# Small parameter loads moved from SP's queue to ACT's, and a new order of the first steps, in a two-layer decoder trunk

## The reference, cut to what matters

```python
for l in range(DEPTH):
    h = rmsnorm(x, g_mix[l])
    z = h @ w_in[l]                      # 1024 x 3080: conv b, c, v; q, k, v; 8 forget logits
    ...
    q = rmsnorm(q, g_q[l]); k = rmsnorm(k, g_k[l])
    log_f = log_sigmoid(f_logit + b_f[l])
    y_fox = forgetting_attention(q, k, v, log_f)
    x = x + concat([y_conv, y_fox]) @ w_out[l]
    m = rmsnorm(mem, g_mem[l])
    x = x + mem_cross_attention(rmsnorm(x, g_xa[l]), m, ...) @ w_xo[l]
    ...                                   # layer 0: dense SwiGLU; layer 1: top-2-of-8 expert SwiGLU
```

## Time and profile before

| | |
|---|---|
| median of 3 runs | 1467.98 us (1465.68 to 1470.63) |
| profiled execution | 1475.52 us, of it 1474.0 us span |
| PE busy | 1396.1 us (95%) |
| DVE, ACT, POOL busy | 1000.9, 803.3, 77.7 us |
| moved by DMA | 386.28 MB, mean 262 GB/s |
| first matmul, first product with a z slot | 13.72 us, 28.26 us |

### The profile page before, as it was taken

How to read it: one execution, slowest core, us unless ns; L and a number is a source line. 1 busy time by engine, 2 the same in 40 slices (tenths; PEclk the granted TensorE clock), 3 DMA queues, 4 the chain that set the end, 5 groups by cost and what they waited for, 6 DMA issues and landing times.

```text
span 1474.0 us, 19381 instructions
## 1 busy us (share of the span) xinstructions
PE 1396.1 (95%) x7593; PEld 1188.5 (81%) x7593; DVE 1000.9 (68%) x779; ACT 803.3 (54%) x702; POOL 77.7 (5%) x82
## 2 busy tenths in 40 slices
PE   5899998999999999985999999999999999999998
PEld 4897666899988997564888888888888888888786
DVE  4437345545457465334798897888878888889888
ACT  4335124334344433223686777777867777677674
POOL 3000000000001000002000000000000000000400
PEclk9999899999999998996999999999999999999999
DMA  9323044464459321413898999999999999999994
GB/s 304 127 88 115 29 172 165 136 208 163 150 200 379 129 87 58 176 56 136 324 388 345 385 346 394 389 341 400 351 380 367 357 393 380 351 382 345 406 399 181
DMA packets 126627, 386.28 MB, mean 262 GB/s; under 512 B 7938, under 2 KB 61806, under 8 KB 126574
## 3 DMA queue, kind: packets, MB, share of 16 engines
q1 hardware_dynamic: 114686, 365.08, 66.5%
q0 software_dynamic: 3168, 11.54, 2.0%
q10 hardware_dynamic: 8720, 8.91, 1.7%
HBM read 369.78 MB, written 15.73 MB: 262 GB/s over the span
## 4 chain that ended last, share of the span: by engine, by line
PE 68%; DVE 11%; DMA 8%; ACT 6%; issue 5%; POOL 1%; SPq 1%; DVEq 0%; ACTq 0%; POOLq 0%
PE bank L1458 41%; PE bank L1454 13%; PE bank L1455 12%; DVE wl L1035 5%; DMA ring<-in_we_gate 4%; DMA ring<-in_we_down 3%; ACT wh L730 3%; DVE wl L1016 2%; PE bank L1860 1%; DVE xl L1041 1%; ACT xh L918 1%; ACT wh_third L730 1%; DMA rows_of<-xn,rows 1%; DVE scratch L1162 1%; DVE scratch L1145 0%
## 5 line engine op out<-in xcount | busy, mean ns | idle before, releaser
L1035 DVE TENSOR_TENSOR wl<-ring,wh 128x2816 fp32r<-128x2816 f32 (+1 forms) x127 | 400.3, 3171 | 61.3 <-PE bank L1458 35.2
L730 ACT ACTIVATE wh<-ring 128x2816 fp32r<-128x2816 f32 (+1 forms) x128 | 336.8, 2633 | 124.8 <-DMA ring<-in_we_down 43.0
L1016 DVE TENSOR_TENSOR wl<-ring,wh 128x3072 fp32r<-128x3072 f32 (+2 forms) x53 | 158.2, 2988 | 101.1 <-ACT wh L716 91.9
L1454 PE MATMUL bank<-wh,xh 128*128 128x512 f32 x528 | 200.9, 381 | 22.0 <-ACT wh L730 14.5
L1035 DVE TENSOR_TENSOR wl<-ring,wh_third 128x2816 fp32r<-128x2816 f32 (+1 forms) x64 | 187.1, 2923 | 33.4 <-PE bank L1458 25.2
L1455 PE MATMUL bank<-wh,xl 128*128 128x512 f32 x528 | 199.2, 377 | 0.0
L1458 PE MATMUL bank<-wl,xh 128*128 128x512 f32 (+1 forms) x768 | 194.9, 375 | 0.0
L730 ACT ACTIVATE wh_third<-ring 128x2816 fp32r<-128x2816 f32 (+1 forms) x64 | 155.7, 2432 | 52.7 <-DMA ring<-in_we_up 21.0
L716 ACT ACTIVATE wh<-ring 128x3072 fp32r<-128x3072 f32 (+1 forms) x52 | 128.3, 2469 | 97.2 <-DMA ring<-in_w_xq 46.4
L1458 PEld LDWEIGHTS bank<-wl,xh 128*128 128x128 f32 x768 | 141.9, 188 | 18.4
L1454 PEld LDWEIGHTS bank<-wh,xh 128*128 128x128 f32 x528 | 99.9, 189 | 44.9 <-issue 19.4
(11 more groups left out here) (271 smaller groups left out, 2032.1 us busy)
## 6 DMA issues: line engine op xcount, KB each, us to landing
ring<-in_we_gate SPq DMA_DIRECT2D x64, 1408.0 KB, 7.9
ring<-in_we_up SPq DMA_DIRECT2D x64, 1408.0 KB, 8.2
ring<-in_we_down SPq DMA_DIRECT2D x56, 1536.0 KB, 9.0
ring<-in_w_in SPq DMA_DIRECT2D x16, 1536.0 KB, 8.8
ring<-in_w_gate SPq DMA_DIRECT2D x6, 1536.0 KB, 7.4
ring<-in_w_up SPq DMA_DIRECT2D x6, 1536.0 KB, 6.7
ring<-in_w_down SPq DMA_DIRECT2D x6, 1536.0 KB, 7.0
rows_of<-zeros ACTq DMA_DIRECT2D x1, 8704.0 KB, 46.2
```

The lines of the kernel that those rows point to most:

```text
L730: nc.scalar.activation(wh_in_pass(j, n), ring[:, slot, 0:n], ACT.Copy).then_inc(high_ready, 1)
L1016: nc.vector.tensor_tensor(wl[:, j, 0:n], ring[:, slot, 0:n], wh[:, j, 0:n].bitcast(F32), ALU.subtract).then_inc(low_ready, 1)
L1035: nc.vector.tensor_tensor(wl[:, j % 2, 0:n], ring[:, j % NSLOT, 0:n], wh_in_pass(j, n).bitcast(F32), ALU.subtract).then_inc(low_ready, 1)
L1454: nc.tensor.matmul(dst, x_high, w_high, start=first, stop=False)
```

## The change

SP's queue now holds x, z0, z1, the memory, z2, z3. The 18 small DMAs are the first instructions of ACT's queue, ahead of the load of its function table. PE transposes x before it waits for the 18 and transposes `vrows`. On ACT the split of z0 comes behind `input_high`, then the squares of x, the split of z1 and the squares of the memory. On DVE the low part of z0 comes first, then the diagonal of the roots (`root_diagonal`), the low part of z1, and the normalising of the memory. The memory's transposes on PE move from ahead of qk0 to behind `roots_spread` after qk1; DVE copies them behind the forget gate's first steps. The names of the banks are put in the new order; with it qk0 and qk1 get other banks, "f" and "qk2" still share one. `memraw` and one of two scratch areas for squares change places.

```diff
@@ -66,9 +66,10 @@
 def layer_results(layer):
 
     names = [f"xT{i}" for i in range(4)] + ["f"]
+    names += ["qk0", "qk1", "rr"]
     if layer == 0:
         names += [f"mT{i}" for i in range(4)]
-    names += ["qk0", "qk1", "rr", "qk2", "qk3", "v0", "v1", "ssqk"]
+    names += ["qk2", "qk3", "v0", "v1", "ssqk"]
     names += [f"conv{i}" for i in range(3)] + [f"bq{i}" for i in range(4)] + [f"conv{i}" for i in range(3, 6)]
     names += [f"s{h}" for h in range(8)]
     names += ["mk0", "mk1", "mv0", "mv1", "ssc", "ssmk"] + [f"pt{h}" for h in range(8)]
@@ -242,13 +243,13 @@
         zc = part(0, 12, S)
         zqk = part(3072, 8, S)
         sq = part(5120, 8, S)
-        memraw = part(5120, TT, D)
+        memraw = part(1024, TT, D)
         sc = part(5120, FH, 3 * P)
         osq = part(5120, TT * FH, HD)
         rdiag = part(12544, TT, P)
         rfull = part(12800, S)
         rsquare = part(13056, S)
-        mixjunk = part(1024, TT, D)
+        mixjunk = [part(5120, TT, D), part(1024, TT, D)]
         xajunk = part(5120, TT, D)
         ffnjunk = part(0, TT, D)
         vtok = part(8192, 2, FH * HD)
@@ -517,25 +518,7 @@
                     slot_free(fill_names[n - NSLOT])
                 dst = ring[:, n % NSLOT, 0:k * c].rearrange("p (k c) -> p k c", k=k)
                 sp.dma_start(dst, src).then_inc(slot_filled[n % NSLOT], 16)
-                if n == 0:
-
-                    for nm, src in (("mix", g_mix), ("xa", g_xa), ("mem", g_mem), ("ffn", g_ffn), ("cv", g_conv_out),
-                                    ("fox", g_fox_out), ("xq", g_xq), ("xk", g_xk)):
-                        r, k = vec[0, nm], L * src.shape[1] // P
-                        sp.dma_start(vrows[r:r + k, :], src.rearrange("l (k p) -> (l k) p", p=P)).then_inc(params_loaded, 16)
-                    r = vec[0, "tap"]
-                    sp.dma_start(vrows[r:r + 12 * L, :], conv_w.rearrange("l j (k p) -> (l j k) p", p=P)).then_inc(params_loaded, 16)
-                    for nm, src in (("q", g_q), ("k", g_k)):
-                        r = vec[0, nm]
-                        for half in range(2):
-                            sp.dma_start(vrows[r:r + L, half * HD:half * HD + HD], src).then_inc(params_loaded, 16)
-                    for l in range(L):
-                        sp.dma_start(wf[:, KT * l:KT * l + KT], w_in[l][:, ICOLS - FH:ICOLS].rearrange("(k p) c -> p k c", p=P)).then_inc(params_loaded, 16)
-                    r = vec[0, "bf"]
-                    sp.dma_start(vrows[r:r + L, :].rearrange("l (a h) -> l a h", h=FH),
-                                 b_f.unsqueeze(1).to_broadcast([L, P // FH, FH])).then_inc(params_loaded, 16)
-                    sp.dma_start(wr[:], w_router[0].rearrange("(k p) c -> p k c", p=P)).then_inc(params_loaded, 16)
-                    sp.dma_start(brow[:], b_router[0:1, :].to_broadcast([P, NE])).then_inc(params_loaded, 16)
+                if n == 1:
                     sp.dma_start(memraw, mem[0].rearrange("(t p) d -> p t d", p=P)).then_inc(mem_loaded, 16)
 
             gu_rows = [w[0].rearrange("e (k p) c -> p (e k) c", p=P) for w in (we_gate, we_up)]
@@ -689,6 +672,23 @@
         @block.scalar
         def _(act):
             steps = [0]
+            for nm, src in (("mix", g_mix), ("xa", g_xa), ("mem", g_mem), ("ffn", g_ffn), ("cv", g_conv_out),
+                            ("fox", g_fox_out), ("xq", g_xq), ("xk", g_xk)):
+                r, k = vec[0, nm], L * src.shape[1] // P
+                nc.scalar.dma_start(vrows[r:r + k, :], src.rearrange("l (k p) -> (l k) p", p=P)).then_inc(params_loaded, 16)
+            r = vec[0, "tap"]
+            nc.scalar.dma_start(vrows[r:r + 12 * L, :], conv_w.rearrange("l j (k p) -> (l j k) p", p=P)).then_inc(params_loaded, 16)
+            for nm, src in (("q", g_q), ("k", g_k)):
+                r = vec[0, nm]
+                for half in range(2):
+                    nc.scalar.dma_start(vrows[r:r + L, half * HD:half * HD + HD], src).then_inc(params_loaded, 16)
+            for l in range(L):
+                nc.scalar.dma_start(wf[:, KT * l:KT * l + KT], w_in[l][:, ICOLS - FH:ICOLS].rearrange("(k p) c -> p k c", p=P)).then_inc(params_loaded, 16)
+            r = vec[0, "bf"]
+            nc.scalar.dma_start(vrows[r:r + L, :].rearrange("l (a h) -> l a h", h=FH),
+                         b_f.unsqueeze(1).to_broadcast([L, P // FH, FH])).then_inc(params_loaded, 16)
+            nc.scalar.dma_start(wr[:], w_router[0].rearrange("(k p) c -> p k c", p=P)).then_inc(params_loaded, 16)
+            nc.scalar.dma_start(brow[:], b_router[0:1, :].to_broadcast([P, NE])).then_inc(params_loaded, 16)
             nc.scalar.preload_act_table_set("natural_log_exp_and_others")
 
             def then_wait(ins):
@@ -753,34 +753,32 @@
 
             for l in range(L):
 
-                if l == 0:
-                    act.wait_ge(x_loaded, 16)
-                else:
+                if l == 1:
                     act.wait_ge(consts_ready, 1)
                     nc.scalar.dma_start(rows_of.rearrange("(p a) (b c) -> p (a b) c", p=P, c=256),
                                         zeros[:].unsqueeze(1).to_broadcast([P, (2 * NE + 1) * (D // 256), 256])
                                         ).then_inc(rows_cleared, 16)
                     nc.scalar.preload_act_table_set("natural_log_exp_and_others")
                     high_of(l, "z", 0)
-                    mean_square(l, 0, "d", mixjunk, 0)
+                    mean_square(l, 0, "d", mixjunk[1], 0)
                 if l == 0:
-                    for t in range(TT):
-                        mean_square(l, t, None, mixjunk, 0)
                     act.wait_ge(params_loaded, 16 * NPARAMS)
                     nc.scalar.activation(wide(wf_wide[0][:, 0]), wf_each(0), ACT.Copy).then_inc(wf_split, 1)
-                    high_of(0, "z", 0)
                     act.wait_ge(*taken(0, "vec"))
                 input_high(l, "xT", "mix")
                 if l == 1:
-                    mean_square(l, 1, "d", mixjunk, 0)
+                    mean_square(l, 1, "d", mixjunk[1], 0)
                     high_of(l, "z", 1)
                 if l == 0:
+                    high_of(0, "z", 0)
+                    for t in range(TT):
+                        mean_square(l, t, None, mixjunk[0], 0)
+                    high_of(0, "z", 1)
                     act.wait_ge(mem_loaded, 16)
                     for t in range(TT):
                         nc.scalar.activation(memT[:].rearrange("p k s -> p (k s)")[:, t * D:t * D + D], memraw[:, t, :],
                                              ACT.Square, scale=D ** -0.5,
                                              accum_out=msq[:, 2 + t:3 + t]).then_inc(meansq_ready, 1)
-                    high_of(0, "z", 1)
 
                 for i in range(4):
                     act.wait_ge(*taken(l, f"qk{i}"))
@@ -1079,16 +1077,13 @@
                     dve.wait_ge(*taken(0, "vec"))
                 input_low(l, "xT", "mix")
                 if l == 0:
+                    low_of(0, "z", 0)
+                    root_diagonal(l, "mix", 0, rdiag)
+                low_of(l, "z", 1)
+                if l == 0:
                     normalise(l, "mem", memraw, 2, memraw)
-                    low_of(0, "z", 0)
-                low_of(l, "z", 1)
-
-                root_diagonal(l, "mix", 0, rdiag)
-                if l == 0:
-                    for i in range(4):
-                        dve.wait_ge(*full(l, f"mT{i}"))
-                        nc.vector.tensor_copy(memT[:, 2 * i:2 * i + 2, :].rearrange("p k s -> p (k s)"), bank(l, f"mT{i}")[:]
-                                              ).then_inc(take(l, f"mT{i}"), 1)
+                else:
+                    root_diagonal(l, "mix", 0, rdiag)
                 for i in range(4):
                     dve.wait_ge(*full(l, f"qk{i}"))
                     nc.vector.tensor_copy(zqk[:, 2 * i:2 * i + 2, :].rearrange("p a s -> p (a s)"), bank(l, f"qk{i}")[:]
@@ -1109,6 +1104,11 @@
                         dve.wait_ge(*taken(l, "rr"))
                         then_wait(nc.vector.reciprocal(erow[:], rsquare[0:16, :]))
                         nc.vector.tensor_scalar(erow[:], erow[:], EPS, None, ALU.mult).then_inc(erow_ready, 1)
+                        if l == 0:
+                            for b in range(4):
+                                dve.wait_ge(*full(l, f"mT{b}"))
+                                nc.vector.tensor_copy(memT[:, 2 * b:2 * b + 2, :].rearrange("p k s -> p (k s)"), bank(l, f"mT{b}")[:]
+                                                      ).then_inc(take(l, f"mT{b}"), 1)
                     if i == 2:
                         dve.wait_ge(fln_ready, l + 1)
                         then_wait(nc.vector.tensor_tensor(fz[:, 3, :], fz[:, 3, :], fz[:, 2, :], ALU.subtract))
@@ -1580,21 +1580,18 @@
                 return i * BANK, min(i * BANK + BANK, DFF)
 
             pe.wait_ge(ident_ready, 1)
-            pe.wait_ge(params_loaded, 16 * NPARAMS)
```

(11 more changed lines are left out.)

## The result

The changed kernel takes 1476.32 us in the median of 5 runs (1475.6 to 1483.29), the kernel before 1467.98 in 5 (1465.68 to 1470.63): a ratio of 1.0062, 95% interval 1.0042 to 1.0082. It is slower by about 8 us. The first median lies in the range that was forecast, the second 1.8 us above it; both say slower, as was forecast.

What follows compares the result with a forecast made beforehand. The prediction took the start of the first z product, qk0, behind the last small DMA's landing as the bound: +11.1 (landing) − 4.4 (order) − 1.0 (clock) = +5.7 us, giving 1473.7 us, range 1462 to 1478.5.

Steps and rivals of the forecast that it cites:

- Part 1: New ACT and DVE order: from T (last small DMA's landing) to qk0 10.24 us instead of 14.68, gaining 4.4 us.
- What was called hidden: Work moved later (squares of x, z1's split, the memory's normalising) is ready before PE needs it, by 3.8 us and more.
- Part 2: PE transposes x while it waits for the parameters: 16 transposes, 3.62 us, gaining nothing alone.
- Part 3: Memory's transposes behind qk1: work time unchanged, PE's hole before qk2 cut from 4.73 to 2.8 us.
- term of −1.0 us for the clock: Shorter hole before qk2 may keep the granted clock up, worth 2.1 us; half taken, ends −2.1 and +2.1.
- new hole ahead of qk0: PE idles some 2.3 us between `forget_rows` and qk0, in place of a hole split in two by the memory's transposes.
- Part 4: Small DMAs on q10 alternate with q1's packets one for one, so their last landing T moves to 24.7, 11.1 us later.
- upper bound: Latest T, once everything on q1 is over: 21.6 us from 3.0 on, 1.9 for small packets and the landing, T = 27.
- lower bound of 12.6: Earliest T, if the tiny packets are not held up at all and ACT's issue starts 1.0 us earlier.
- the small packets slip through: Rival at the DMA engines: many tiny descriptors go in one turn, T 12.6, total 5.4 to 7.5 us faster; chance 0.20.

Runs made afterwards that it cites:

- r1: The changed kernel run again unaltered, in a later set on the same chip as three others: 1480.31 us, ratio 1.0069 to the kernel before.
- e2: Changed kernel with its 18 small DMAs back on SP's queue and the memory ahead of z1 again, new order of work kept: 1463.66 us, ratio 0.9959 to before.
- e3: Changed kernel plus one wait: SP issues x and z0, then waits for the 18 small DMAs before z1: 1464.95 us, ratio 0.9965 to before.
- e4: Changed kernel with `wr`, `brow` and layer 1's forget columns issued last on ACT's queue, on their own semaphore: 1471.64 us, ratio 1.0021 to before.
- e5: New order with small DMAs on SP's queue, plus bank names exchanged so qk3, not qk2, shares bank f: 1460.37 us, ratio 0.9934 to before.
- e6: New order with small DMAs on SP's queue, but `wr`, `brow` and layer 1's forget columns behind z3 on their own semaphore: 1461.53 us, ratio 0.9941 to before.
- e7: New order, SP's queue with 15 small DMAs behind z0 and 3 behind z3, and qk3 in bank f: 1459.46 us, ratio 0.9923 to before.
- e8: Changed kernel with only two bank names exchanged, so qk3, not qk2, shares bank f: 1477.37 us, ratio 1.0055 to before.
- r3: Rerun in the later set of the new order with the small DMAs on SP's queue: 1463.04 us, ratio 0.9946 to before.
- r2: Rerun in the later set of the changed kernel with qk3 instead of qk2 in bank f: 1473.63 us, ratio 1.0031 to before.
- e1: Kernel before with only the 18 small DMAs moved to ACT's queue, old order of computation: 1486.86 us, ratio 1.0116 to before.
- r4: Rerun in the later set: new order, SP's queue with 3 small DMAs behind z3, qk3 in bank f: 1461.86 us, ratio 0.9943 to before.

## Why the prediction was right

It forecast 1473.7 us, range 1462 to 1478.5, slower the likeliest; the measured median is 1476.32, 2.6 us above. That it is so near is in part luck: the trace was off by more (see the sum below), and r1's median lies 1.8 us outside the range. Step by step:

- **Part 1, the order on ACT and DVE**: 10.24 us from T to qk0 were forecast, 10.1 measured, in the changed kernel as in e2, e3, e4, e5, e6, e7 and e8. The gain of 4.4 was 4.6, and e2 shows it by itself. What was called hidden was hidden.
- **Part 2**: x is transposed at 6.21 to 9.85, and it changes nothing, as said.
- **Part 3**: a hole of 2.8 us was forecast, 2.98 came, ended by L1098, the read of "f". The transposes cost PE nothing. The term of −1.0 us for the clock came out as +0.7 (10.34 us late at 121 us, after 9.67 at qk0): in the profiled execution the clock fell, and the 96 matmuls behind the hole took 14.48 us instead of 13.84. The term rested on a wrong reading. A mean of 0.55 between 1.0 and 0.5 puts the fall at 43.10 and not at 43.45, so it came 2.6 us after PE had stopped, not 3.0, and the row spoke against a hole of 2.8 us keeping the clock up; in the changed kernel it fell 2.4 us after PE had stopped. Behind the same hole it stayed up in e2, e4, e6, r1 and r3, so a chance was the right form for this term, though not for the reason given. The new hole ahead of qk0, put at 2.3 us, was 1.36: `forget_rows` took 5.5 us, not under 5.
- **Part 4, T**: the mechanism was right, turns one for one by number, and so was the length of the train of tiny packets: 16.2 us were worked out from `wf`'s first packet to the end, and it ran from 10.8 to 27.0. The term that was mis-sized is its start. I had `wf` moving at 8.0, 1.9 us behind its issue as x had been; it was issued at 6.56, not 6.06, and moved at 10.8. T = 27.83 is therefore 3.1 us past the 24.7 forecast: 2.8 from the start, 0.3 from the landing (0.8 us instead of 0.5). It is 0.8 past what I had called the upper bound: q1 moved from 2.9 to 27.0, 24.1 us where the bound had 23.5 (21.6 for the bytes, 1.9 for the tiny packets), and the landing adds its 0.3. So the train and q1 ended together; by this count a still later start would hardly have moved T. A smaller slip: the 9.4 ns of a tiny packet alone come from a microsecond that was not full, with 1222 of the 1711 packets in its first half (6.5 ns each); in turns a pair took 73.8 ns (433 and 436 in 2 us on 16 engines), 10.5 more than the large packet alone.

The sum of the trace's terms is then +14.3 − 4.6 + 0.7 = +10.4 us at the 121 us mark, where +5.7 were forecast. The medians say +8.3, 10.5 in the set of r1.

DMA views of the changed kernel, 6 to 10 us, the stretch in which `wf` was expected to begin, and its DMA list of the same stretch (us to landing at the end):

```profile
q1 hardware_dynamic: 965, 1.46, 102.2%
q10 hardware_dynamic: 165, 0.04, 4.8%
...
ring<-in_w_in SPq DMA_DIRECT2D x2, 1536.0 KB, 17.7
scratch<-in_mem SPq DMA_DIRECT2D x1, 1024.0 KB, 15.4
wf<-in_w_in ACTq DMA_DIRECT2D x2, 32.0 KB
```

q10 moves only 165 packets in 4 us there, those of the row loads ahead of `wf`, while q1 moves 965. It is not the turns that hold q10 back in this stretch, for with work at hand it would have had as many. In e3, where SP issues only x and z0, they run from about 9.65 us, 3.4 us behind `wf`'s issue instead of 4.2 (in e4, e8, r1 and r2 it is 4.0 to 4.2 again). So a part of the late start (0.8 us) goes with what SP has issued; the other 1.5 us stays without it, and I have no run that says where it lies. It may also be why T in e3, 13.78, was no better than by SP alone, and above the lower bound of 12.6 that the prediction gave for packets that nothing holds up; no run separates that.

Of the rivals, "the small packets slip through" falls with the equal counts, at three pairs of sizes now (1536 bytes beside 1024, 1536 beside 32, 4096 beside 32). The Trainium skill, "DMA: Bandwidth & Descriptors", section "Queues, rings and completion order", has an engine take a whole group of descriptors from one queue before it turns to the next; the counts over two microseconds can't show the size of a group, only that both queues get the same number. Its section "Issuing engines are not separate DMA queues" says that a second issuing engine saves issue time and no more. The trace agrees as far as e3 goes, whose T is within 0.2 us of e2's, but not even the issue time came back there; and it says nothing of a price, which e1 shows: T 14.3 us later by the move alone.

## What to carry to other kernels

Before small loads are moved to a second queue, count their packets, not their bytes: as long as the first queue has work, each packet waits for one of the first queue's, here 63 ns for 1536 bytes, and 200 of them per engine were 13 us of waiting for 100 KB. Small loads that everything waits for belong ahead of the large ones on the same queue, or the large ones must wait (e3), and loads that are first used much later need a count of their own. When a hole in PE ends with a read of a PSUM bank, look first at which later result was given that bank; here one exchanged name removes it.

## What the runs showed of the hardware that I had not expected

- A DMA's issue on ACT or SP takes longer when much is waiting in its queue. `b_f` behind two loads of 1024 packets took 1.96 us (before), 3.19 (e3), 5.11 (changed kernel); behind one such load, in e4, 0.49. ACT was not free for computation until 19.55 us in the changed kernel, which would have cost time had T been earlier.
- The granted clock after a hole is not a property of the kernel. Behind the same idle time of 2.98 us before qk2 it fell in the changed kernel and in e3, and stayed up in e2, e4, e6, r1 and r3. With 4.73 us, in before and e1, it fell both times. Before qk0 PE had idled for 1.8 to 2.5 us in e3, e5, e6, r1 and r3, and the clock fell between 0.6 us before qk0's start and 1.0 us behind it; it was granted in full from qk0 on where PE had idled for 1.4 to 1.5 us (the changed kernel, e2, e4, e7, e8, r2, r4), though in the changed kernel and e8 it had only risen within that idle time. In e3, e6, r1 and r3 it had risen three to four microseconds before qk0, in e5 it had been up since before 13 us, so a clock that has only just risen is not what these have in common. A fall cost 1.2 to 1.5 us over the next 96 matmuls before qk0, and 2.1 to 2.7 before qk2 (13.84 us in before, 13.94 in e1, 14.34 in e3, 14.48 in the changed kernel, instead of 11.8). Over a whole execution it shows too: of the changed kernel's five, the two longest (1480.82 and 1483.29 us) have mean granted clocks of 0.964 and 0.971, the other three 0.975 and 0.976. That all of the difference is the clock is not shown.
